# Two blocks of a transformer, expert stages: the down matrix read in 16 KB rows, and the up products taken from every fourth column

## What is computed

```python
def expert_block(args):
    toks, e = args
    xb = x[toks]
    hb = jax.nn.silu(xb @ w1[e]) * (xb @ w3[e])
    return hb @ w2[e]
```

## Time and profile before

| what | value |
|---|---|
| median of 3 runs | 1777.34 us (1777.30 to 1782.64) |
| the profiled execution's own time | 1774.95 us |
| its span, first to last instruction | 1773.1 us |
| mean granted clock of TensorE | 0.915 of full |
| TensorE busy | 1459.3 us, 82% of the span |
| VectorE, ScalarE busy | 630.9 us, 257.4 us |
| moved by DMA | 528.65 MB in 155,838 packets |
| first expert stage, by its up products | 218.5 to 739.3 us of the span |
| second expert stage, likewise | 1293.9 to 1756.1 us |

### The profile page before, as it was taken

One profiled execution on the slowest core, in us unless ns is written; L12 is line 12 of the kernel. 1 busy time (PEld: TensorE's weight loads), 2 busy tenths in 40 slices (PEclk: granted clock), 3 DMA queues, 4 the chain that ended last, 5 costly groups with the idle time before them and its releaser, 6 DMA issues. The chain is left out here.

```text
span 1773.1 us, 28921 instructions
## 1 busy us (share of the span) xinstructions
PE 1459.3 (82%) x12551; PEld 970.0 (55%) x12551; DVE 630.9 (36%) x1742; ACT 257.4 (15%) x532; POOL 43.0 (2%) x63
## 2 busy tenths in 40 slices
PE   7999788988878897699998998998876666666665
PEld 6545445656555564379766846886443333333333
DVE  3523444212132332314755733332352222222223
ACT  2421331111011111122100212221100000000000
POOL 1000000000000000010100100000000000000000
PEclk9999889999889998889999999998888888888887
DMA  9678589999999999963233241432669999999995
GB/s 340 233 260 332 149 319 414 410 414 413 411 411 409 412 410 421 356 198 104 89 107 107 74 167 68 142 109 90 260 272 421 420 421 421 420 421 421 419 421 238
DMA packets 155838, 528.65 MB, mean 298 GB/s; under 512 B 38888, under 2 KB 57520, under 8 KB 139328
## 3 DMA queue, kind: packets, MB, share of 16 engines
q1 hardware_dynamic: 152080, 522.93, 75.2%
q0 software_dynamic: 1200, 3.77, 0.6%
q10 hardware_dynamic: 2432, 0.10, 0.1%
HBM read 525.71 MB, written 1.06 MB: 297 GB/s over the span
## 5 line engine op out<-in xcount | busy, mean ns | idle before, releaser
L1373 PE MATMUL ps<-weight_ring,e_xT 128*32 128x256 f32 x4096 | 308.7, 468 | 203.9 <-DMA weight_ring<-in_w_up_dram 138.5
L1373 PEld LDWEIGHTS ps<-weight_ring,e_xT 128*32 128x32 f32 x4096 | 173.1, 134 | 336.4 <-issue 289.2
L1405 PE MATMUL ps<-weight_ring,e_gT 128*32 128x256 f32 x2048 | 125.5, 386 | 17.6 <-DVE e_gT L1635 17.6
L1633 DVE TENSOR_TENSOR e_g<-e_act_g,ps 128x128 f32<-128x128 f32 x64 | 18.4, 288 | 268.1 <-ACT e_act_g L1461 267.0
L1461 ACT ACTIVATE e_act_g<-ps 128x128 f32<-128x128 f32 x64 | 17.8, 278 | 602.2 <-PE ps L1373 602.2
L1405 PEld LDWEIGHTS ps<-weight_ring,e_gT 128*32 128x32 f32 x2048 | 60.4, 110 | 68.6 <-DVE e_gT L1635 28.7
L1632 DVE TENSOR_TENSOR e_act_g<-e_act_g,ps 128x128 f32<-128x128 f32 x32 | 9.2, 288 | 219.4 <-ACT e_act_g L1461 219.2
L969 PE MATMUL ps<-e_nT,e_ctx_w 128*128 128x256 f32 x320 | 74.1, 391 | 5.2 <-DVE e_ctx_gcols L1069 3.4
L1353 PE MATMUL ps<-e_y,e_GwT 32*128 32x256 f32 x1056 | 75.6, 400 | 2.4 <-DVE e_y L1659 1.8
L1340 PE MATMUL ps<-e_n,e_Gt 128*32 128x256 f32 x1056 | 71.0, 385 | 5.9 <-DVE e_Gt L1572 5.9
L969 PEld LDWEIGHTS ps<-e_nT,e_ctx_w 128*128 128x128 f32 x320 | 62.2, 197 | 14.8 <-issue 3.6
(11 more groups left out here) (498 smaller groups left out, 1924.5 us busy)
## 6 DMA issues: line engine op xcount, KB each, us to landing
weight_ring<-in_expert_w_dram SPq DMA_DIRECT2D x96, 2048.0 KB, 20.7
weight_ring<-in_w_down_dram SPq DMA_DIRECT2D x32, 2048.0 KB, 24.6
weight_ring<-in_w_gate_dram SPq DMA_DIRECT2D x32, 2048.0 KB, 19.4
weight_ring<-in_w_up_dram SPq DMA_DIRECT2D x32, 2048.0 KB, 23.9
weight_ring<-in_w_in_dram SPq DMA_DIRECT2D x26, 2048.0 KB, 8.6
weight_ring<-in_w_ada_dram SPq DMA_DIRECT2D x12, 2048.0 KB, 8.1
e_ctx_w<-in_w_in_dram SPq DMA_DIRECT2D x18, 1024.0 KB, 23.1
weight_ring<-in_w_out_dram SPq DMA_DIRECT2D x4, 2048.0 KB, 10.2
```

The costliest lines, as they stand in the source:

```text
L1373: mm = pe.matmul(ps[32 * j:32 * j + 32, 4, 0:256].rearrange("p (w f) -> p w f", w=2), xT[:, k % 2, k // 2, :], w13[:, :, k, j * P:(j + 1) ...
L1405: mm = pe.matmul(ps[32 * m:32 * m + 32, 5, 0:256], gT[:, j * 32:(j + 1) * 32], w2[:, j, m * 256:(m + 1) * 256], start=(j == 0), stop=(j == ...
```

## The change

The down matrix is loaded like the other two: partition `p` gets the rows `4p` to `4p + 3`, 16 KB in one piece. Row `4p + j` then lies in partition `p` at piece `j`. For the down products to stay right, group `j` of the up products has to make the hidden columns `j`, `4 + j`, `8 + j` and so on. So its moving operand takes every fourth column of `w1` and `w3`, each element 16 bytes behind the last. The results lie in the same places of PSUM, in the new order of columns.

```diff
     slot = 3 * u + which
     if which == 2:
-        dst = c.ring[:, slot, :].rearrange("p (o k n) -> p o k n", o=1, k=KF)
-        src = W[2][0, e].rearrange("o (k p) f -> p o k f", p=P)
+        src = W[2][0, e].rearrange("o (p k) f -> p o (k f)", k=KF)
     else:
-        dst = c.ring[:, slot, :].rearrange("p (o n) -> p o n", o=1)
         src = W[which][0, e].rearrange("o (p k) f -> p o (k f)", k=KD)
-    sp.dma_start(dst, src).then_inc(sems[slot], 16)
+    sp.dma_start(c.ring[:, slot, :].rearrange("p (o n) -> p o n", o=1), src).then_inc(sems[slot], 16)
...
                 for k in range(KD):
                     for j in range(4):
                         mm = pe.matmul(ps[32 * j:32 * j + 32, 4, 0:256].rearrange("p (w f) -> p w f", w=2),
-                                       xT[:, k % 2, k // 2, :], w13[:, :, k, j * P:(j + 1) * P],
+                                       xT[:, k % 2, k // 2, :], w13[:, :, k, j::4],
                                        start=(k == 0), stop=(k == KD - 1))
```

## The result

After the change the kernel takes 1812.28 us (median of 4 runs, 1808.74 to 1813.44), beside 1777.32 us for the kernel before on the same chip (4 runs, 1776.33 to 1782.64): a ratio of 1.0189, 95% interval 1.0171 to 1.0206. It is slower by 35.0 us. The forecast was 1805 us, with a range of 1753 to 1860 us.

A forecast was written before the change was run, and what follows sets the result against it. The weight stream was taken to bound both expert stages, with TensorE overtaking it in the first: +36.1 us there and -5.8 us in the second, +30.3 us on 1774.95 us, giving 1805 us (whole range 1753 to 1860 us).

The forecast's parts named there:

- What bounds the kernel: Both expert stages: the weight stream sets the pace; TensorE has little room in the first, much in the second.
- The price of a group: Up products, both stages: a group of 64 TensorE instructions goes from 3.64 to 7.28 us; likeliest case 6.6 to 8.9, chance 0.44.
- ScalarE's added time: Up group priced by ScalarE's 0.97 ns more per stepped element: 7.60 us, total +41.1 us (1816 us).
- VectorE's row: Up group priced by VectorE's 0.31 ns more per stepped element: 4.93 us, total 1756 us; within the faster rival, chance 0.33.
- The first stage: First expert stage: groups take 99.5 us more against 63.4 us of waiting, so TensorE becomes the bound: +36.1 us.
- The three experts: First expert stage, cross-check: three experts take 52.4 us instead of 51.2 us.
- The second stage: Second expert stage: the stream stays the bound, -9.4 us from rows and +3.6 us from exposed groups: -5.8 us.
- The exposed ends: Second expert stage: first and last up groups are exposed whole, 7.28 - 5.60 and 7.28 - 5.35, together +3.6 us.
- the row term: Down-matrix loads: 16 KB rows save 0.31 us per matrix, 30 matrices a stage: -9.4 us where the stream bounds.
- The free step: Up products: the stepped read costs nothing, both stages stay stream-bound, -18.8 us, 1756 us; faster rival, chance 0.33.
- The colliding readers: Up products: four column groups queue on the same 16 bytes, 14.6 us per group, about 2190 us; chance 0.17.
- The point of no change: Whole kernel: the step's price meets the rows' gain at 6.39 us per group; no-change rival, chance 0.06.

The follow-up runs named there:

- rows_only: Against the changed kernel: down matrix still in 16 KB rows, but up products read neighbouring columns, pairing hidden columns wrongly; 1766.04 us, ratio 0.9925 to the kernel before.
- dose4: Against the changed kernel: only the first four of eight k steps read every fourth column, the others neighbours; 1773.0 us, ratio 0.9966 to the kernel before.
- probe_readers: Against the kernel before: half the up products left out, one column group reading neighbours, then one and two reading at 16-byte steps; 1810.62 us in a single run.
- dose6: Against the changed kernel: only the first six of eight k steps read every fourth column, the others neighbours; 1783.62 us, ratio 1.0035 to the kernel before.

## Why the prediction was right, and what was off in it

**What bounds the kernel.** Right. A longer up group showed in the first stage and not in the second, and the waits for weights fell from 63.4 us to nothing in the one and from 138.5 to 72.1 us in the other.

**The price of a group.** 7.28 us was taken, 7.46 us measured, inside the likeliest case's 6.6 to 8.9. ScalarE's added time (7.60 us) was the nearest end, its factor (6.77 us) was too low, and VectorE's row (4.93 us) was far below; why VectorE pays less for its step stays open. That a group which runs partly at half clock would take no less was also right, and more: it takes no longer either. Windows of single groups of this line, two of the changed kernel, then two of the kernel before (matmuls, weight loads, clock, DMA):

```profile
1399.40:1407.00 7.60, 7.46 (x64) 2.47 (x64) 0.78 1.01 427
...
1429.00:1436.50 7.50, 7.46 (x64) 2.32 (x64) 1.00 1.00 422
```

```profile
1306.10:1309.80 3.70, 3.64 (x64) 1.95 (x60) 1.00 0.99 425
...
1524.10:1530.70 6.60, 6.51 (x64) 3.31 (x64) 0.55 1.05 436
```

A mean of 0.78 is partly 1.2 GHz, partly 2.4 GHz, and the group takes the same 7.46 us as at 2.4 GHz throughout. The starts of the single instructions in the two traces show it without a mixture. In the changed kernel a step of 256 elements takes 0.453 us in the median of the 822 that lie wholly in stretches at 2.4 GHz, and 0.453 us in that of the 110 at 1.2 GHz. In the kernel before these are 0.216 and 0.427 us. So where the clock is low the stepped read costs almost nothing more. That is why the groups grew by only 64 us in the second stage, where many ran at 1.2 GHz, and by 105 us in the first.

**The first stage.** 36.1 us forecast, 39.6 us measured. By its own terms: the groups grew by 238.6 - 133.5 = 105.2 us, the waits of 63.4 us went, and what is left of the stage's length, which holds all the other work and waits of TensorE, is 2.2 us less; this last term is only the remainder. 105.2 - 63.4 - 2.2 = 39.6. The missing 3.5 us are 32 x 0.18 us of group price, less those 2.2. The three experts were forecast at 52.4 us and took 52.6.

**The second stage.** -5.8 us forecast, -2.4 us measured. The exposed ends are right: 7.47 - 5.60 and 7.44 - 5.35 make +4.0, beside +3.6. What was mis-sized is the row term, "-9.4 us": rows_only gives -6.4 us here and -5.5 us in the first stage. The step of the prediction that failed is the last of that term, "0.32 us less, and 0.31 us less in time at the share of 1.01". It divides the two rates of the earlier trace rows by their shares, 102.8% and 101.1%, and then sets one share for both. The packets' own time was nearly right: between 1400 and 1700 us one of 4 KB takes 163.4 ns in the mean before, and one of 16 KB 617 ns after, so that four short ones are 654 ns. But short packets overlap more. Over the steady second stage the packets' time per engine was 1.013 of the stretch before and 1.005 after, and so part of the gain is not one in time. The rates of the earlier trace rows as they stand have this in them: 2.097 MB at 411 and at 431 GB/s are 5.102 and 4.865 us, 0.237 us less, or 7.1 us for 30 matrices. In rate:

```profile
1400.00:1740.00 340.00, 223.16 (x2922) 126.14 (x2926) 89.12 (x312) 14.56 (x44) 0.00 (x0) 0.84 1.01 420
```

That is the window of the kernel before; the changed one moves 426 GB/s in 1400:1785 (above). For 6.29 MB per expert that is 14.98 and 14.77 us, 0.21 us less, and the periods fell by 0.21 (15.09 to 14.88). 30 x 0.21 = 6.3, beside the 6.4 of rows_only.

**The sum.** +30.3 us forecast. The two misses, +3.5 and +3.4, make 37.2, and the spans differ by 37.4. The forecast was counted from the profiled execution's 1774.95 us, so its distance to the measured 1812.28 is 7.3 us; against the median before, the change costs 35.0 us.

**The rivals.** The free step (1756 us) is out: 0.455 us where 0.215 would be free. VectorE's price (4.93 us) is out for the step of 16 bytes, though a price of that size would probably not have been quite free either: dose4 at 5.54 us still gained, but only 4.9 us, where rows_only gained 11. The rival left out, as the forecast did, that the waits lie unevenly in the first stage. The colliding readers (2190 us) are out by probe_readers. The point of no change was put at 6.39 us per group; between dose4 (-0.34% at 5.54) and dose6 (+0.35% at 6.50) it lies at some 6.0 us, lower because the row term was smaller and the knee is round.

## What to carry to other kernels

A layout that makes a transfer's rows longer is paid by whoever reads the result: price that read per 16-byte line that it touches, not only per element (shown here for TensorE's moving operand in fp32), and count it on the engine that has the least room in each stage. Idle time on that engine absorbs a longer step only where it lies; sum it over halves of a stage before spending it. A new order of columns is cheaper to make once, on a small product and an idle engine (here 64 products of 128 x 128 on VectorE), than on the moving operand of a large one.

## What the runs showed of the hardware that was not expected

- TensorE's moving read of 4-byte elements has a floor of 1.77 ns per 16-byte line (0.453 us for 256 lines), beside 0.84 ns per element for neighbours. Two elements in a line are enough, adjacent or not; 12 bytes lie between (0.335 us).
- The floor does not depend on the granted clock (0.453 us per step at 1.2 and at 2.4 GHz, where neighbours take 0.427 and 0.216 us), nor on how many column groups read at once (one, two or four: 0.45 us), nor on whether they read the same line or lines far apart (0.454 and 0.455 us in the median).
- 16,384 fewer packets per stage gave 5.5 and 6.4 us (420 to 426 GB/s in the second). The time of single packets promises more (654 ns for four of 4 KB, 617 ns for one of 16 KB), but short ones overlap more (a share of 1.013 before, 1.005 after).
